# Last mixer's output projection: three of its four units with each 128-row product as two 64-row products in separate banks

## Chip, cores and metric

The kernel runs on one core of one Trainium2 chip. What counts is the time of one execution in microseconds (us), as the median of several. In the profile PE is TensorE's matmul stream and PEld its weight loads, DVE is VectorE, ACT ScalarE, POOL GpSimd, and SP the engine that issues the weight DMAs.

## What is computed

Three blocks run one after another on 512 tokens of width 1024, in f32: two of a first model (`even` mixer, FFN, `mla` mixer, FFN) and one of a second. The change is in the last mixer, of the second model:

```python
mix = jnp.concatenate([y_rwkv, o.reshape(B, S, DIFF_DIM)], axis=-1).astype(h.dtype)
h = h + rms_norm(mix @ w_out[l], ln_attn_post[l])
hn = rms_norm(h, ln_ffn_pre[l])
u = causal_dwconv(hn @ w_up[l], conv_w[l], conv_b[l])
gate, val = jnp.split(u, 2, axis=-1)
f = (jax.nn.gelu(gate, approximate=True) * val) @ w_down[l]
h = h + rms_norm(f, ln_ffn_post[l])
```

`mix @ w_out` is the output projection, 512 x 1024 by 1024 x 1024. The norm behind it needs the sum of squares over all 1024 features of a token, so nothing of the FFN can begin before the last column of the projection is there.

## The kernel before

Everything is held with features on the partitions: `XH` and `XL` are [128, 8 slices, 512 tokens]. A matrix product in f32 is made of three products in fp32r: weights and activations are each split into a high part and the rest, and `w_hi*XH + w_hi*XL + w_lo*XH` is summed in one PSUM bank. Weights come in units of 1 MB (`w_raw`, two slots): for the projection a unit is 1024 rows by 256 columns, so there are four units of two tiles (t = 0, 1) of 128 output features, and tiles n = 0 to 7 in all. One tile is 8 slices k times 3 factors = 24 products of 128 rows by 128 columns with 512 streamed tokens.

The order of the work is written out by hand, one program for each engine, with semaphores between them:

- SP loads unit u as soon as the low part of unit u - 2 is split off.
- ACT makes `w_hi` (L1036, 128x2048) of unit u + 1, once the unit's slot has been read (`read_of`), then takes the squares of the two tiles of unit u (`mean_square`, L1043), which wait for `lin_free`. In the last unit it makes one more high part between the two squares: the own weights of the FFN's second unit (`own_split`, L1080).
- DVE makes `w_lo` of unit u + 1 (L1582) from `w_hi`, then copies the two tiles of unit u from their banks to `Y2` (L2253) and raises `lin_free`. In the last unit its part of `own_split` (L2260) stands between the two copies.
- PE computes tiles 0 and 1 inside `group_norm` (L3298), then tiles 2 to 7 in `linear` (L2475), each through `feature_tile` (L2425), in banks L % 4, that is 0 to 3 by turns. `unit(u)` waits for `w_lo`, and `free(L)` for the bank.
- POOL adds the squares up (L886, L889), all but the last tile's.

Behind the last tile PE sums the squares over the partitions with a matrix of ones: L3093 for POOL's sum, L3095 for the last tile's squares. ACT turns this into `rstd` (L1084, L1085). DVE scales and adds the residual (L1970, L1973), ACT and DVE split the normed value (L1055, L1589), and PE begins the FFN (L2872). Eight records of L2861 ahead of it are four products that are never read.

Each engine takes its instructions in order, and ACT and DVE wait where they stand. The two lines around which the change is made:

```python
dve.wait_ge(lin_ready, L + 1)
dve.tensor_copy(Y2[:, n, :], bank[L % 4][:, :]).then_inc(lin_free, 1)
```

`side(h)` is a slice of 64 partitions: `side(0)` is 0 to 63, `side(1)` 64 to 127. Elsewhere the kernel has products on such halves in plain f32, among them L3113 in `lora_up`: 64 rows by 128 columns, 512 streamed, rows 0-63 and 64-127 by turns, each into another bank than the one before.

Of the kernel before, what the change touches and what calls it, by code (L numbers as in the profile page):

```python
# [13 lines left out]
ALU = mybir.AluOpType  # L14
AX = mybir.AxisListType

P = 128
SEQ = 512
D = 1024
KT = D // P  # L20
# [147 lines left out]
def build(nc, d, out, scratch, stages):  # L168
    units, first = units_of(stages, d)
# [17 lines left out]
    with ExitStack() as ctx:  # L187
        def sb(name, shape, dt=F32):
            return ctx.enter_context(nc.sbuf_tensor(name, shape, dt))

        def sem(name):
            return ctx.enter_context(nc.semaphore(name))

        bank = [ctx.enter_context(nc.psum_tensor(f"bank{i}", [P, 512], F32)) for i in range(8)]
# [6 lines left out]
        XH = sb("XH", [P, KT, SEQ], F32R)  # L201
        XL = sb("XL", [P, KT, SEQ], F32R)
# [82 lines left out]
        lin_ready = sem("lin_ready")  # L285
        lin_act = sem("lin_act")
        lin_free = sem("lin_free")
# [151 lines left out]
        Y2 = region(KT * SEQ, KT, SEQ)  # L439
# [170 lines left out]
        def wv(u, n, kt):  # L610

            return [w[:, u % 2, 0:kt * n].rearrange("p (t n) -> p t n", n=n) for w in (w_hi, w_lo)]
# [78 lines left out]
        def tok_units(stage):  # L691
            return [u for u in range(NU) if units[u][0] == stage]
# [32 lines left out]
        def side(h):  # L725
            return slice(CH * h, CH * (h + 1))
# [19 lines left out]
        inv = nc.dram_tensor("inverse_blocks", (3, P, BL * BL), F32, kind="Internal").ap()  # L746

        VAR, GATE = (4, 5), (6, 7)
        CENTRE = (4, 5, 7, 4)
        ABANK = (7, 5, 7, 6)  # L750
        PRE = (4, 5, 7, 4, 5, 7, 4, 5)
# [816 lines left out]
        def _(dve):  # L1568
# [7 lines left out]
            def split(u):  # L1576

                if u >= NU:
                    return
                dve.wait_ge(w_hi_ready, units_split(u + 1))  # L1580
                for (to, frm), (hi, _) in zip(split_pieces(u, w_raw, w_lo), split_pieces(u, w_raw, w_hi)):
                    last = dve.tensor_tensor(to, frm, hi.bitcast(F32), ALU.subtract)  # L1582
                last.then_inc(w_lo_ready, 1)
# [571 lines left out]
            def mix2():  # L2155
                L = lin_base["mix2"]
# [3 lines left out]
                for u in tok_units("rwkv_in"):  # L2160
# [15 lines left out]
                    for t in range(2):  # L2176
                        j = 2 * i + t
# [54 lines left out]
                for j in range(4):  # L2232
                    value(j)
                    dve.wait_ge(rw_vm, j + 1)
                    dve.scalar_tensor_tensor(vv[:, j, :], bank[CENTRE[j]][:, :], -1.0 / 64, vv[:, j, :],
                                             ALU.mult, ALU.add).then_inc(rw_vc, 1)
# [11 lines left out]
                for u in tok_units("mix_out"):  # L2248
                    split(u + 1)
                    for t in range(2):  # L2250
                        n = 2 * (u - first["mix_out"]) + t
                        dve.wait_ge(lin_ready, L + 1)
                        dve.tensor_copy(Y2[:, n, :], bank[L % 4][:, :]).then_inc(lin_free, 1)  # L2253
                        L += 1
                        if t == 0 and u == tok_units("mix_out")[-1]:
                            own_split(u + 2)
# [147 lines left out]
        def _(pe):  # L2404
# [60 lines left out]
            def free(L):  # L2465
                if L >= 4:
                    pe.wait_ge(lin_free, L - 3)

            def unit(u):
                pe.wait_ge(w_lo_ready, u + 1)  # L2470
# [4 lines left out]
            def linear(stage, L, release=False, late=None, skip=0):  # L2475

                for u in tok_units(stage)[skip:]:
                    unit(u)
                    for t in range(2):
                        free(L)  # L2480
                        if late and u == first[stage] and t == 0:
                            hi, lo = wv(u, 256, KT)
                            rows, name = late[1], late[0]
                            pe.wait_ge(ot_lo, ot_base[name] + min(rows.values()) - 1)
                            for p, k in enumerate([k for k in range(KT) if k not in rows] + list(rows)):
                                if k in rows:
                                    pe.wait_ge(ot_lo, ot_base[name] + rows[k])
                                for j, (w, x) in enumerate(((hi, XH), (hi, XL), (lo, XH))):
                                    m = pe.matmul(bank[L % 4][:, :], w[:, k, 0:P], x[:, k, :],
                                                  start=(p == 0 and j == 0), stop=(p == KT - 1 and j == 2))  # L2490
                            m.then_inc(lin_ready, 1)
                            L += 1
                            continue
                        m = feature_tile(u, KT, 256, whole(P * t), P, 0, L,
                                         release=release and t == 1 and u == tok_units(stage)[-1])
                        m.then_inc(lin_ready, 1)
                        L += 1
                return L
# [540 lines left out]
            def mix2():  # L3039
                L = lin_base["mix2"]  # L3040
                pe.wait_ge(down_added, down_base["ffn1"] + 4)
                for u in tok_units("rwkv_in"):
                    j = u - first["rwkv_in"]
                    unit(u)
                    if j == 0:
                        feature_pair(u, 256, (whole(0), whole(P)), L, "pre")
                        L += 2
                    else:
                        for t in range(2):
                            free(L)  # L3050
                            feature_tile(u, KT, 256, whole(P * t), P, 0, L).then_inc(lin_ready, 1)
                            L += 1
                            if j == 1 and t == 0:
                                pe.wait_ge(down_added, down_base["ffn1"] + KT)
                                pe.wait_ge(rstd_ready, norm_use["pre"])
                                pe.wait_ge(sq_mixed, 1)
                                pe.matmul(bank[5][:, :], C("ones"), sq_acc, start=True, stop=True).then_inc(ss_first, 1)
                                pe.matmul(bank[7][:, :], C("ones"), sq_acc2, start=True, stop=True).then_inc(ss_ready, 1)
                    if j == 2:
                        pe.wait_ge(first_rstd, 1)  # L3060
                        columns("pre")
                for u in tok_units("diff_in"):
                    j = u - first["diff_in"]
                    unit(u)
                    for t in range((2, 2, 2, 2, 4, 4)[j]):
                        free(L)
                        if j < 4:
                            feature_tile(u, KT, 256, whole(P * t), P, 0, L).then_inc(lin_ready, 1)
                            if t == 0 and j == 0:
                                lora_up()  # L3070
                            if t == 1:
                                key_sums(j)
                        else:
                            token_tile(u, KT, 256, lambda w, k: w[:, k, :], 256, 0, t, L).then_inc(lin_ready, 1)
                            if j == 4:
                                value_mean(t)
                            if j == 5 and t == 0:
                                pe.wait_ge(rw_vc, 4)
                            if j == 5 and t < 2:
                                inner(2 * t)  # L3080
                                inner(2 * t + 1)
                        L += 1
                    if j == 5:
                        pe.wait_ge(rw_ak, 4)
                pe.wait_ge(lin_free, L)
                pe.wait_ge(alibi_loaded, 16 * 16)
                attention("diff")
                rwkv_chunks()
                group_norm(L)
                linear("mix_out", L + 2, skip=1)  # L3090
                pe.wait_ge(rstd_ready, norm_use["post"])
                pe.wait_ge(sq_used, all_summed("post"))
                pe.matmul(bank[7][:, :], C("ones"), sq_acc, start=True, stop=False)  # L3093
                pe.wait_ge(sq_ready, LAST_POST + 1)
                pe.matmul(bank[7][:, :], C("ones"), squares[:, LAST_POST % 3, :], start=False, stop=True)\  # L3095
                    .then_inc(ss_ready, 1)

            def value_mean(t):
                if t == 2:
                    pe.wait_ge(rw_max, 4)  # L3100
                if t == 3:
                    pe.wait_ge(rw_vc, 1)
                pe.matmul(bank[CENTRE[t]][:, :], C("half_ones"), vv[:, t, :], start=True, stop=True).then_inc(rw_vm, 1)

# [220 lines left out]
            for j in range(3):  # L3325
                m = pe.transpose(bank[0][:, P * j:P * (j + 1)], vrow[:, j, :], ident)
# [34 lines left out]
```

## Time and profile before

| | us |
|---|---|
| median of 3 runs | 1925.27 |
| lowest, highest | 1925.08, 1927.24 |
| span of the profiled execution | 1924.0 |
| PE under way | 1890.1 (98%) |
| DVE busy | 999.1 (52%) |
| ACT busy | 740.1 (38%) |

For the profiled execution the span is given alone, from its first to its last instruction; what lies around it is not. The median of the runs is 1.3 us above it. The projection's tiles 2 to 7 run from 1511.40 to 1544.20 us of the span, and the FFN's first product starts at 1551.94. PE's busy time is that in which a product is under way: products overlap, so that the time shown for one is longer than the distance from one start to the next. Plain f32 products appear as two records each (two passes), fp32r ones as one.

### The profile page before, as it was taken

The numbers are of one execution on the slowest core, as the hardware profiler recorded it, in microseconds if no ns is written. First come the engines' busy times: TensorE is split into PE (matmuls) and PEld (weight loads), VectorE is DVE, ScalarE is ACT, GpSimd is POOL, SyncE is SP. The second block draws the span as 40 slices with busy tenths as digits, with TensorE's granted clock in tenths as the row PEclk, the third lists the DMA queues.
The fourth block names the chain that finished last, engine by engine and source line by source line (L and its number), as shares of the span: only waits on it lengthen the run. The fifth ranks groups of instructions, "written<-read, shape, count | busy, mean of one in ns | idle before, by whom it ended". The sixth has DMA issues, their size and how long they took to land.

```text
span 1924.0 us, 26779 instructions
## 1 busy us (share of the span) xinstructions
PE 1890.1 (98%) x10729; PEld 1527.6 (79%) x10729; DVE 999.1 (52%) x1418; ACT 740.1 (38%) x1111; POOL 179.1 (9%) x215
## 2 busy tenths in 40 slices
PE   9999999999999999999999999999999999999998
PEld 7875788888888777788888888777878778888887
DVE  5456453434325686553343434749563566656523
ACT  4247432222224575542222323554342454333322
POOL 1001210000001100010000000303551100000001
PEclk9999999999999999999999999999999999999999
DMA  6310133232322202123223232321120223232321
GB/s 201 105 44 1 50 99 98 87 109 87 105 92 80 72 23 66 45 91 105 91 87 109 88 109 87 100 88 44 24 67 25 88 77 109 87 108 89 107 90 66
DMA packets 137795, 158.74 MB, mean 83 GB/s; under 512 B 15976, under 2 KB 125552, under 8 KB 137712
## 3 DMA queue, kind: packets, MB, share of 16 engines
q1 hardware_dynamic: 136272, 155.01, 25.2%
q0 software_dynamic: 1440, 2.58, 0.5%
q8 instruction: 58, 0.95, 0.2%
q14 instruction: 25, 0.20, 0.0%
HBM read 153.89 MB, written 3.68 MB: 82 GB/s over the span
## 4 chain that ended last, share of the span: by engine, by line
PE 90%; DVE 6%; ACT 2%; issue 1%; DMA 0%; SPq 0%; POOL 0%; ACTq 0%; DVEq 0%
PE bank L2893 35%; PE bank L2926 16%; PE bank L2425 13%; PE bank L2450 3%; PE bank L2980 2%; PE bank L2569 2%; PE bank L2944 2%; PE bank L2839 1%; PE bank L2872 1%; PE bank L2597 1%; PE bank L2688 1%; PE bank L2584 1%; PE bank L2511 1%; PE bank L2541 1%; DVE XL L1589 1%
## 5 line engine op out<-in xcount | busy, mean ns | idle before, releaser
L2893 PE MATMUL bank<-XH,w_hi 128*128 128x512 f32 x992 | 386.8, 390 | 0.7 <-DVE arena L1889 0.7
L2893 PE MATMUL bank<-XL,w_hi 128*128 128x512 f32 x992 | 386.0, 389 | 0.0
L2893 PE MATMUL bank<-XH,w_lo 128*128 128x512 f32 x992 | 385.9, 389 | 0.0
L2893 PEld LDWEIGHTS bank<-XH,w_hi 128*128 128x128 f32 x992 | 186.2, 188 | 39.9 <-DVE arena L1889 0.9
L2893 PEld LDWEIGHTS bank<-XL,w_hi 128*128 128x128 f32 x992 | 186.2, 188 | 39.1 <-issue 0.5
L2893 PEld LDWEIGHTS bank<-XH,w_lo 128*128 128x128 f32 x992 | 186.2, 188 | 38.8
L2425 PE MATMUL bank<-XH,w_hi 128*128 128x512 f32 x448 | 178.7, 399 | 2.5 <-DVE w_lo L1582 2.4
L2425 PE MATMUL bank<-XH,w_lo 128*128 128x512 f32 x448 | 175.3, 391 | 0.0
L2425 PE MATMUL bank<-XL,w_hi 128*128 128x512 f32 x448 | 175.1, 391 | 0.0
L1582 DVE TENSOR_TENSOR w_lo<-w_raw,w_hi 128x2048 fp32r<-128x2048 f32 (+5 forms) x67 | 116.4, 1757 | 93.9 <-ACT w_hi L1036 93.5
L1936 DVE TENSOR_TENSOR w_lo<-w_raw,w_hi 128x2048 fp32r<-128x2048 f32 x24 | 55.0, 2292 | 174.2 <-ACT w_hi L1347 174.2
L1036 ACT ACTIVATE w_hi<-w_raw 128x2048 fp32r<-128x2048 f32 (+5 forms) x67 | 96.6, 1464 | 106.8 <-PE bank L2425 44.7
L2926 PE MATMUL bank<-XH,w_hi 128*128 128x512 f32 x320 | 124.5, 389 | 0.0
L2926 PE MATMUL bank<-XH,w_lo 128*128 128x512 f32 x320 | 124.5, 389 | 0.0
L2926 PE MATMUL bank<-XL,w_hi 128*128 128x512 f32 x320 | 124.5, 389 | 0.0
L1900 DVE TENSOR_TENSOR arena<-bank,arena 128x512 f32<-128x512 f32 x66 | 45.5, 690 | 141.0 <-PE bank L2893 141.0
L1291 ACT ACTIVATE w_hi<-w_raw 128x2048 fp32r<-128x2048 f32 x32 | 61.3, 1917 | 147.5 <-PE bank L2893 147.5
L1347 ACT ACTIVATE w_hi<-w_raw 128x2048 fp32r<-128x2048 f32 x24 | 46.0, 1917 | 187.1 <-PE bank L2926 166.5
L1876 DVE TENSOR_TENSOR w_lo<-w_raw,w_hi 128x2048 fp32r<-128x2048 f32 x33 | 75.6, 2290 | 62.9 <-ACT w_hi L1311 56.0
L2425 PEld LDWEIGHTS bank<-XH,w_hi 128*128 128x128 f32 x448 | 84.5, 189 | 25.1 <-DVE w_lo L1582 4.9
L2425 PEld LDWEIGHTS bank<-XL,w_hi 128*128 128x128 f32 x448 | 84.5, 189 | 18.9 <-issue 1.7
L2425 PEld LDWEIGHTS bank<-XH,w_lo 128*128 128x128 f32 x448 | 84.5, 189 | 17.8
(459 smaller groups left out, 3336.1 us busy)
## 6 DMA issues: line engine op xcount, KB each, us to landing
w_raw<-in_ffn_w_gate SPq DMA_DIRECT2D x22, 1024.0 KB, 5.3
w_raw<-in_ffn_w_up SPq DMA_DIRECT2D x22, 1024.0 KB, 5.3
w_raw<-in_ffn_w_down SPq DMA_DIRECT2D x22, 1024.0 KB, 4.9
w_raw<-in_w_up SPq DMA_DIRECT2D x22, 1024.0 KB, 5.1
w_raw<-in_w_in SPq DMA_DIRECT2D x13, 1024.0 KB, 5.3
w_raw<-in_w_down SPq DMA_DIRECT2D x11, 1024.0 KB, 5.0
w_raw<-in_even_w_in SPq DMA_DIRECT2D x8, 1024.0 KB, 5.3
w_raw<-in_even_w_out SPq DMA_DIRECT2D x4, 1024.0 KB, 5.3
```

The lines of the kernel that those rows point to most:

```text
L1036: last = act.activation(to, frm, ACT.Copy)
L1291: act.activation(w_hi[:, (u0 + 1) % 2, :], w_raw[:, (u0 + 1) % 2, :], ACT.Copy).then_inc(w_hi_ready, 1)
L1347: act.activation(w_hi[:, slot, :], w_raw[:, slot, :], ACT.Copy).then_inc(w_hi_ready, 1)
L1582: last = dve.tensor_tensor(to, frm, hi.bitcast(F32), ALU.subtract)
L1876: dve.tensor_tensor(w_lo[:, a, :], w_raw[:, a, :], w_hi[:, a, :].bitcast(F32), ALU.subtract).then_inc(w_lo_ready, 1)
L1900: dve.tensor_tensor(to[:, c, :], bank[2 + c][:, :], rstd, ALU.mult).then_inc(u_out, 1)
L1936: dve.tensor_tensor(w_lo[:, slot, :], w_raw[:, slot, :], w_hi[:, slot, :].bitcast(F32), ALU.subtract).then_inc(w_lo_ready, 1)
L2425: m = pe.matmul(bank[to][0:M, :], cols(w, k), x[:, x0 + k, :], start=(first_k and k == 0 and j == 0), stop=(last_k and k == kt - 1 and j = ...
L2450: m = pe.matmul(bank[to][:, 0:N], x[:, x0 + k, s * P:(s + 1) * P], cols(w, k), start=(k == 0 and j == 0), stop=(k == kt - 1 and j == 2))
L2569: pe.matmul(bank[SCORE[g % 4]][:, c:c + P * nk], qc[:, h, P * i:P * (i + 1)], kc[:, h, P * k0:P * (k0 + nk)], start=True, stop=True)
L2893: m = pe.matmul(bank[b][:, :], w[:, k, P * c:P * (c + 1)], x[:, k, :], start=(k == 0 and j == 0), stop=(k == KT - 1 and j == 2))
L2926: m = pe.matmul(bank[p][:, :], left, right, start=False, stop=(stop and c == 1 and j == 2))
```

## The change

For tiles 2 to 7 (the three units behind the first), `linear` gives way to `mix_out_halves`. Each product of 128 rows becomes two of 64: one on rows 0 to 63, into bank L % 4 as before, and one on rows 64 to 127, into a second bank (`LOWER`, 4, 5 or 6 by turns). The two orders of k and of the three factors are kept, and the two halves follow one another. DVE copies the upper half's bank to `Y2` and then adds the lower half's bank to it; between the two stands `link`, a wait of DVE for its own copy. `lin_free` is raised by the addition. From n = 5 on PE also waits until tile n - 3 has left its lower bank. Tiles 0 and 1 are as before.

```diff
+        LOWER = (4, 5, 6)
...
                         dve.wait_ge(lin_ready, L + 1)
-                        dve.tensor_copy(Y2[:, n, :], bank[L % 4][:, :]).then_inc(lin_free, 1)
+                        if n < 2:
+                            dve.tensor_copy(Y2[:, n, :], bank[L % 4][:, :]).then_inc(lin_free, 1)
+                        else:
+                            link(dve.tensor_copy(Y2[:, n, :], bank[L % 4][:, :]))
+                            dve.tensor_tensor(Y2[:, n, :], Y2[:, n, :], bank[LOWER[n % 3]][:, :], ALU.add)\
+                               .then_inc(lin_free, 1)
...
-                linear("mix_out", L + 2, skip=1)
+                mix_out_halves(L + 2)
...
+            def mix_out_halves(L):
+
+                for u in tok_units("mix_out")[1:]:
+                    unit(u)
+                    hi, lo = wv(u, 256, KT)
+                    for t in range(2):
+                        n = 2 * (u - first["mix_out"]) + t
+                        free(L)
+                        if n >= 5:
+                            pe.wait_ge(lin_free, L - 2)
+                        for k in range(KT):
+                            for j, (w, x) in enumerate(((hi, XH), (hi, XL), (lo, XH))):
+                                for r, to in ((side(0), L % 4), (side(1), LOWER[n % 3])):
+                                    m = pe.matmul(bank[to][:, :], w[r, k, P * t:P * (t + 1)], x[r, k, :],
+                                                  start=(k == 0 and j == 0), stop=(k == KT - 1 and j == 2))
+                        m.then_inc(lin_ready, 1)
+                        L += 1
```

On DVE, the program of before from tile 4's copy to the norm (the buffer `arena` holds `Y2`; L1582 is `w_lo` of the FFN's first unit, L2260 the own weights):

```order
L2253 COPY arena<-bank 128x512 x2
L1582 TENSOR_TENSOR w_lo<-w_raw,w_hi 128x2048
L2253 COPY arena<-bank 128x512
L2260 TENSOR_TENSOR under_arena<-w_raw,under_arena 128x2048
L2253 COPY arena<-bank 128x512
L1970 SCALAR_TENSOR_TENSOR arena<-arena,vec 128x512
```

and the changed program at the same place (its lines are 1 to 6 further down):

```order
L2257 COPY arena<-bank 128x512
L2258 TENSOR_TENSOR arena<-arena,bank 128x512
L2257 COPY arena<-bank 128x512
L2258 TENSOR_TENSOR arena<-arena,bank 128x512
L1583 TENSOR_TENSOR w_lo<-w_raw,w_hi 128x2048
L2257 COPY arena<-bank 128x512
L2258 TENSOR_TENSOR arena<-arena,bank 128x512
L2266 TENSOR_TENSOR under_arena<-w_raw,under_arena 128x2048
L2257 COPY arena<-bank 128x512
L2258 TENSOR_TENSOR arena<-arena,bank 128x512
L1971 SCALAR_TENSOR_TENSOR arena<-arena,vec 128x512
```

An addition stands behind each copy; nothing else has changed its place. On PE, the program of before where tile 1 ends and tile 2 begins:

```order
L3298 MATMUL bank<-XH,w_hi 128x512
L3298 MATMUL bank<-XL,w_hi 128x512
L3298 MATMUL bank<-XH,w_lo 128x512
L2425 MATMUL bank<-XH,w_hi 128x512
L2425 MATMUL bank<-XL,w_hi 128x512
L2425 MATMUL bank<-XH,w_lo 128x512
```

and the changed one (the shape is that of the output, 128 features by 512 tokens):

```order
L3322 MATMUL bank<-XH,w_hi 128x512
L3322 MATMUL bank<-XL,w_hi 128x512
L3322 MATMUL bank<-XH,w_lo 128x512
L3117 MATMUL bank<-XH,w_hi 128x512 x2
L3117 MATMUL bank<-XL,w_hi 128x512 x2
L3117 MATMUL bank<-XH,w_lo 128x512 x2
```

Each of the 144 rows of tiles 2 to 7 has become a pair at the same place.

## Rows read from the trace of the kernel before

**Rows 1.** The page, part 4: shares by engine of the chain that ended last

```profile
PE 90%; DVE 6%; ACT 2%; issue 1%; DMA 0%; SPq 0%; POOL 0%; ACTq 0%; DVEq 0%
```

**Rows 2.** That chain from 1505 to 1552: start us, us, what

```profile
1511.40 22.09 PE bank L2425 x96
...
1533.52 0.70 DVE arena L2253
...
1534.78 1.91 ACT w_hi L1036
...
1536.71 2.29 DVE w_lo L1582
...
1542.16 2.29 DVE under_arena L2260
...
1545.13 0.64 ACT arena L1043
...
1545.81 1.14 PE bank L3095 x2
```

**Rows 3.** Timeline of PE: start, us, line, operation, tiles, shapes, count [idle before <-releaser]

```profile
1543.74 0.39 PE L2425 MATMUL bank<-XL,w_hi 128*128 128x512 f32 x1
1543.97 0.40 PE L2425 MATMUL bank<-XH,w_lo 128*128 128x512 f32 x1
1544.20 1.02 PE L3093 MATMUL bank<-arena,con 128*128 128x512 f32 x2
1545.81 1.13 PE L3095 MATMUL bank<-arena,con 128*128 128x512 f32 x2 [0.59 <-ACT arena L1043]
1546.77 3.60 PE L2861 MATMUL bank<-con 128*128 128x512 f32 x8
1551.94 0.50 PE L2872 MATMUL bank<-XH,w_hi 128*128 128x512 f32 x1 [1.57 <-DVE XL L1589]
```

**Rows 4.** Timelines of PE and of PEld, the 64-row products of L3113

```profile
1287.32 1.98 PE L3113 MATMUL bank<-arena 64*128 64x512 f32 x6
...
1287.32 0.30 PEld L3113 LDWEIGHTS bank<-arena 64*128 64x128 f32 x4 [0.40 <-ACT arena L1444]
...
1289.69 0.29 PEld L3113 LDWEIGHTS bank<-arena 64*128 64x128 f32 x2 [1.22 <-ACT arena L1448]
```

**Rows 5.** Timeline of PE, and a window's row with PEclk, the granted clock

```profile
1212.47 0.50 PE L2425 MATMUL bank<-XH,w_hi 128*128 128x512 f32 x1 [1.79 <-DVE w_lo L1582]
...
1213.19 0.63 PE L2425 MATMUL bank<-XH,w_lo 128*128 128x512 f32 x1
...
1215.75 0.63 PE L2425 MATMUL bank<-XH,w_lo 128*128 128x512 f32 x1
...
1212.90:1216.20 3.30, 3.30 (x10) 2.52 (x9) 2.89 (x5) 3.01 (x5) 3.30 (x8) 0.50 0.81 236
```

**Rows 6.** DVE: a group, one line's min/median/max ns, and two timeline rows

```profile
L2253 DVE COPY arena<-bank 128x512 f32<-128x512 f32 x8 | 5.4, 689 | 9.4 <-PE bank L2425 9.4
...
L1900 DVE TENSOR_TENSOR arena<-bank,arena x66: 680/692/693, 278.1 to 1797.4; 128x512 f32<-128x512 f32 x66
...
1548.36 0.75 DVE L1970 SCALAR_TENSOR_TENSOR arena<-arena,vec 128x512 f32<-128x512 f32 x1 [3.26 <-ACT arena L1085]
1549.14 0.69 DVE L1973 TENSOR_TENSOR X<-X,arena 128x512 f32<-128x512 f32 x1
```

**Rows 7.** Timeline of PE at two other idle times

```profile
182.55 0.69 PE L2632 MATMUL bank<-con,arena 128*128 128x128 f32 x2 [2.70 <-POOL arena L910]
183.03 1.91 PE L2620 MATMUL bank<-arena 128*128 128x512 f32 x2
...
1337.24 1.13 PE L3121 MATMUL bank<-arena,con 128*128 128x512 f32 x2 [1.67 <-ACT arena L1457]
```

**Rows 8.** Timeline of PE and PEld within tile 6: a product and the next one's load

```profile
1534.90 0.39 PE L2425 MATMUL bank<-XL,w_hi 128*128 128x512 f32 x1
1534.90 0.19 PEld L2425 LDWEIGHTS bank<-XH,w_lo 128*128 128x128 f32 x1
```

## The prediction, made before the changed kernel ran

> **What bounds the kernel now.** I read the page first. TensorE (PE) holds 90% of the chain of work that ended last [rows 1], so PE's time in a stage is normally the stage's time, and the first question is what two half-height products cost in place of a full one. The second is which engine releases PE behind this stage, and there the page's average misleads. The chain in order of time [rows 2] shows that the projection is PE-bound only to tile 5: from 1511.40 the 96 products of tiles 2 to 5 take 22.09 us, 0.230 each. At 1533.52 the chain leaves PE. It then runs ACT and DVE by turns: DVE's copy of tile 5, ACT's square of it and its w_hi split, DVE's w_lo split, copy and square of tile 6, the two splits of the own weights (the second at 1542.16), copy and square of tile 7, and only then PE's L3095 at 1545.81. PE is busy all that time with tiles 6 and 7, but it ends them at the same moment as DVE ends L2260 (L3093, behind the last product, starts at 1544.20, and the split begun at 1542.16 ends 2.29 later, at 1544.45). So **two paths end level**: PE's last 48 products, and a serial walk over ACT and DVE. Behind L3095 comes the norm's chain (ACT, then DVE L1970, L1973, L1589), and PE's next real product starts at 1551.94 [rows 3].
>
> One product now starts every 0.227 us (1543.74, 1543.97, 1544.20 [rows 3]), though each is shown as 0.39 long, since records overlap.
>
> **Part 1, the products.** 144 products of 128 rows (3 units, 2 tiles, 8 slices, 3 factors) become 144 pairs with 64 rows each; the streamed columns, 512, stay. A 64-row product is no shorter than a 128-row one, so the pair costs what one did if both halves run at once, and twice that if they take turns. The trace has one place with this shape: L3113, 64 rows by 128 columns, 512 streamed, rows 0-63 and 64-127 by turns, in separate banks; it is in plain f32, so each product is two passes. Serial passes of this size: two take 1.02 us (L3093) and eight 3.60 (L2861), so one follows another after 0.43 and the last lasts 0.59 [rows 3]. The first three products of L3113, six passes, take 1.98 us [rows 4]. In series they would need 5 x 0.43 + 0.59 = 2.7 us before the first load; with the first two products at once they need 0.10 (load) + 3 x 0.43 + 0.59 = 1.98. The loads say the same: four of them cover 0.30 us, no more than the 0.29 of two loads for a lone product; one load is 0.19 [rows 8], so a second follows after 0.10. So the halves do run at once, loads too. What this place does not show is fp32r: there a column is streamed at twice the pace of a pass in f32 (0.227 against 0.43 for 512), and two banks would be written at that pace.
>
> I take a pair at 0.227, the value nearest to L3113. The low bound is 0.214 (half of the 0.427 between starts at half clock, six steps from 1213.19 to 1215.75 [rows 5]), the high bound for halves that do run together 0.24 (0.227 plus a second start some 0.01 behind). Only 96 pairs, those of tiles 2 to 5, lie on the path, as long as the walk over ACT and DVE is the longer one behind them: -1.3 to +1.3 us, taken as 0. Entering and leaving the half-array form may cost up to 0.18 (0.39 - 0.21, the tail of one product) once on the path; taken as 0.
>
> The Trainium skill (TensorE: Matmul & The Clock Gate, Part 3) puts it as a span of one matmul plus about 4 ns for each further tile, and says that a small-K matmul takes as long as a full one, the gain being concurrency alone. By that figure, an estimate, 96 pairs would add 0.4 us. No row here shows it for fp32r.
>
> **Part 2, the second bank's drain.** Tiles 2 to 7 now get a copy of one bank and then an addition of the other. The copy is 0.69 us and the addition too (L1900, same shape and sources, 692 ns); between an instruction and one that waits for its result lie 0.03 us (L1970 ends 1549.11, L1973 starts 1549.14) [rows 6]. So 0.72 us for each tile on DVE, 4.3 us in all. For tiles 2, 3 and 4 it is hidden: DVE idles 9.4 us in all ahead of two copies (those of tiles 3 and 5) [rows 6], and a w_lo split ends 5.5 us after its tile (1533.52 to 1536.71 + 2.29 [rows 2]), where PE's next unit wants it only after 48 x 0.227 = 10.9. For **tiles 5, 6 and 7 it is not hidden**, because ACT takes its work in order. ACT's square of tile 5 waits for the addition, the w_hi split stands behind the square, DVE's w_lo split waits for w_hi, tile 6's copy stands behind w_lo, and so on to L3095 [rows 2]. Each addition is one more link in that walk: 3 x 0.72 = **+2.2 us** at L3095. PE's level path gives it no cover; those 2.2 us are new idle time of PE. Counting only the last tile's addition would give +0.7, and would be wrong if the walk is as serial as the rows show.
>
> POOL's sum up to tile 6 is later by the same 1.5 us and still ends before PE comes to L3093. SP's load behind own_lo is later too, but PE has the first four FFN tiles ahead before it wants it. Both at nothing.
>
> **Part 3, the added wait.** From n = 5 on PE waits until tile n - 3 has left its lower bank. A tile lasts 5.4 us and DVE is behind by at most 2.2 us: the wait never holds. 0.
>
> **Part 4, PE's clock.** PE now idles 0.59 us ahead of L3095 [rows 3]; with part 2 it is 2.8 us. In this trace idle times of 1.79 us (before 1212.47) and 2.70 (before 182.55) went with a fall of the granted clock to 0.50, that is 1.2 GHz: the window behind the one shows it, and behind the other two f32 passes take 1.91 us. One of 1.67 us (before 1337.24) did not: two passes there take 1.13, a first load included [rows 5, 7]. So a fall here is more likely than not. What it costs: L3095 alone is on the path (the fill products L2861 end 1.57 us before L2872 needs PE), and its two f32 passes take 1.91 us at half clock (183.03) against 1.02: +0.9 if the fall covers them, 0 if it comes too late. I take half, +0.45.
>
> **The sum.** 0 + 2.2 + 0 + 0.45 = +2.6 us on the profiled span of 1924.0, or 1926.7. The median of the three runs is 1.3 above that span, which I carry over: **1927.9 us**. With the bounds (-1.3 to +1.3, 0 to 0.2, clock 0 to 0.9) this case spans 1926.2 to 1929.9. A measurement of this kernel can tell about 0.2% (3.9 us) from no change, so +2.6 us counts as "same".
>
> **Rivals.**
> *Halves in turn.* The fp32r halves do not overlap, for instance because the output path takes one full-speed stream only. Then a pair is 0.454 and the 144 pairs add 32.7 us; PE's path becomes the longer one, and only the last addition stands behind it (+0.7): 1925.3 + 33.4 = **1958.7, slower**. For it: L3113 streams at half this pace, so the trace has no pair at full pace. Against it: six passes in 1.98 us. It decides from 0.04 us more for each pair (96 x 0.04 = 3.8). This is also the case in which the change does not do what it says. 0.13.
> *Loads in turn.* Only the weight loads of the halves fall behind each other in full, 2 x 0.188 = 0.376 for a pair [rows 8]: 144 x 0.149 = 21.5, and +0.7: 1947.5. Against it: four loads in 0.30 us [rows 4]. Partial forms lie between 0.24 and 0.376; at 0.26 the sum is 1931. 0.07.
> *The pause between products goes.* If the 0.013 us between 0.227 and 0.214 are an unhidden bit of the weight swap, which two independent halves cover for one another, tile 5 is ready 96 x 0.013 = 1.3 us sooner: 1926.6. For it: twice 0.227 would be 0.454, and at half clock the step is 0.427 [rows 5], so the pause is no array time. Against it: each half swaps just as often. It lies inside the main case's bounds and is counted there.
> The Trainium skill (same page, Part 3) says that a weight load overlaps matmuls in flight only where the row groups differ, which would make the halves a gain. Here a full-height load starts together with a full-height product (both at 1534.90 [rows 8]), so the trace contradicts that as written.
> *Slack in the walk.* The additions at tiles 5 and 6 are absorbed, and only the last is paid: 1925.3 + 0.7 = 1926.0. Nothing in the rows offers that slack. 0.05.
> *A real gain* needs pairs under 0.164 us (96 x 0.063 = 6.0, less 2.2), below what 512 columns take at full clock. 0.02.
>
> **How the numbers follow.** Main case 0.73 (of it 0.06 above 1929.1, where bounds add up). Faster 0.02; slower 0.13 + 0.07 + 0.06 = 0.26; same 0.72. The range runs from 1925.8, under the slack case, to 1932, over the main case's top and the mild partial forms; it leaves out the serial cases.
>
> **What would show it.** Pairs: starts of the two halves within 0.01 us, pairs 0.227 apart, tile 5's copy still near 1533.5; 0.45 apart means the serial rival. Drain: six DVE additions of 0.69 us, ACT's w_hi at 1535.5, own_lo at 1543.6, the second ones product at 1548.0 instead of 1545.8, the first FFN product at about 1554.1 to 1555. Clock: a dip to 0.5 near 1547 to 1552. I am wrong if the fp32r halves are not concurrent, or if ACT's square does not stand between DVE's addition and the next split.

## The result and the profile after

| | before | changed |
|---|---|---|
| median of 20 runs, us | 1925.11 | 1927.57 |
| lowest, highest | 1922.21, 1927.24 | 1925.7, 1929.92 |
| span of the profiled execution | 1924.0 | 1926.0 |

The ratio is 1.0014, 95% interval 1.0009 to 1.002: the changed kernel is slower by 1.7 to 3.9 us, clearly there and under the 0.2% that count as a difference here. The forecast was 1927.9.

Spans differ by things that have nothing to do with the change, so the stage is read by itself. **S** is the time from the first product of tile 2 to the FFN's first product: 1511.40 to 1551.94 before, 40.54 us [rows 2, 3], and 1510.40 to 1554.00 in the changed kernel, 43.60. The stage is longer by 3.06 us. Behind S the spans have 372.1 and 372.0 us; ahead of it the changed kernel's execution is 1.0 us quicker, which is why its span is 2.0 and not 3.06 longer.

The chain that ended last in the changed kernel (start us, us, what; `...` stands for short pieces left out):

```profile
1510.40 22.12 PE bank L3117 x192
...
1532.54 0.70 DVE arena L2257
...
1533.26 0.70 DVE arena L2258
...
1534.52 1.91 ACT w_hi L1037
...
1536.46 2.29 DVE w_lo L1583
1538.75 0.61 DVE arena L2257
...
1539.39 0.70 DVE arena L2258
...
1540.65 1.92 ACT under_arena L1081
...
1542.58 2.29 DVE under_arena L2266
1544.88 0.61 DVE arena L2257
...
1545.51 0.70 DVE arena L2258
1546.21 0.02 issue
1546.23 0.64 ACT arena L1044
...
1546.92 2.09 PE bank L3101 x2
```

The first line answers the first of [rows 2]: 192 half products (96 pairs) in 22.12 us, where 96 whole ones took 22.09. From there the walk over DVE and ACT is that of before with three new pieces of 0.70 us (L2258). From tile 2's first product to the last ones product it was 34.41 us (1545.81 - 1511.40), and is 36.52.

PE's timeline at the same place, to be read against [rows 3], and a window's row (PEclk is the third last number):

```profile
1542.99 0.39 PE L3117 MATMUL bank<-XH,w_lo 64*128 64x512 f32 x2
1543.31 1.13 PE L3099 MATMUL bank<-arena,con 128*128 128x512 f32 x2
1546.92 2.08 PE L3101 MATMUL bank<-arena,con 128*128 128x512 f32 x2 [2.48 <-ACT arena L1044]
1548.78 4.12 PE L2867 MATMUL bank<-con 128*128 128x512 f32 x8
1554.00 0.50 PE L2878 MATMUL bank<-XH,w_hi 128*128 128x512 f32 x1 [1.09 <-DVE XL L1590]
...
1546.50:1549.80 3.30, 2.88 (x4) 1.34 (x5) 0.00 (x0) 1.10 (x3) 0.00 (x0) 0.50 0.90 306
```

PE comes to the first ones product 32.91 us after the stage's start (1543.31), before 32.80. Of the 0.11 us, 0.02 belong to the pairs (the last one starts after 32.59 us, the last whole product of before after 32.57) and 0.09 to the change back from halves: L3099 starts 0.32 behind the last pair, where 0.23 lay between the two before. PE then idles 2.48 us ahead of L3101 where it idled 0.59; the granted clock is 0.50 there, which is 1.2 GHz, and the two passes of L3101 take 2.08 us instead of 1.13. So the 3.06 us are 2.11 of walk (36.52 - 34.41) and 0.95 of clock.

The halves themselves, in the middle of a tile:

```profile
1512.14 0.40 PE L3117 MATMUL bank<-XL,w_hi 64*128 64x512 f32 x2
1512.38 0.39 PE L3117 MATMUL bank<-XH,w_lo 64*128 64x512 f32 x2
1512.60 0.40 PE L3117 MATMUL bank<-XH,w_hi 64*128 64x512 f32 x2
```

Each row holds two products, and the two together last 0.39 to 0.40, as one does. Pairs follow one another after 0.22 to 0.24.

### The profile page after: what moved, and what is told of

Its sections match the earlier page's. It is cut to its first block, busy times and chain, and to the rows that moved or that the text cites. A ratio compares the mean times of both kernels' runs of the same rounds, so it can differ in the third digit from the quotient of the medians.

```text
span 1926.0 us, 27075 instructions
## 1 busy us (share of the span) xinstructions
PE 1889.0 (98%) x10873; PEld 1525.7 (79%) x10873; DVE 1002.4 (52%) x1424; ACT 739.8 (38%) x1111; POOL 178.9 (9%) x215
## 4 chain that ended last, share of the span: by engine, by line
PE 90%; DVE 6%; ACT 2%; issue 1%; SPq 0%; DMA 0%; POOL 0%; DVEq 0%; ACTq 0%
PE bank L2899 35%; PE bank L2932 16%; PE bank L2431 12%; PE bank L2456 3%; PE bank L2986 2%; PE bank L2575 2%; PE bank L2950 2%; PE bank L3117 1%; PE bank L2845 1%; PE bank L2878 1%; PE bank L2603 1%; PE bank L2694 1%; PE bank L2590 1%; PE bank L2517 1%; PE bank L2547 1%
## 5 line engine op out<-in xcount | busy, mean ns | idle before, releaser
L2899 PE MATMUL bank<-XH,w_hi 128*128 128x512 f32 x992 | 386.8, 390 | 0.7 <-DVE arena L1890 0.7
L2899 PE MATMUL bank<-XH,w_lo 128*128 128x512 f32 x992 | 385.9, 389 | 0.0
L2899 PE MATMUL bank<-XL,w_hi 128*128 128x512 f32 x992 | 385.9, 389 | 0.0
L2899 PEld LDWEIGHTS bank<-XH,w_hi 128*128 128x128 f32 x992 | 186.2, 188 | 39.8 <-DVE arena L1890 0.9
L2899 PEld LDWEIGHTS bank<-XL,w_hi 128*128 128x128 f32 x992 | 186.2, 188 | 39.2 <-issue 0.5
L2899 PEld LDWEIGHTS bank<-XH,w_lo 128*128 128x128 f32 x992 | 186.2, 188 | 38.7
L2431 PE MATMUL bank<-XH,w_hi 128*128 128x512 f32 x400 | 159.4, 398 | 2.5 <-DVE w_lo L1583 2.4
L2431 PE MATMUL bank<-XH,w_lo 128*128 128x512 f32 x400 | 155.8, 390 | 0.0
L2431 PE MATMUL bank<-XL,w_hi 128*128 128x512 f32 x400 | 155.8, 390 | 0.0
L2932 PE MATMUL bank<-XH,w_hi 128*128 128x512 f32 x320 | 124.5, 389 | 0.0
L2932 PE MATMUL bank<-XH,w_lo 128*128 128x512 f32 x320 | 124.5, 389 | 0.0
L2932 PE MATMUL bank<-XL,w_hi 128*128 128x512 f32 x320 | 124.5, 389 | 0.0
L1901 DVE TENSOR_TENSOR arena<-bank,arena 128x512 f32<-128x512 f32 x66 | 45.5, 690 | 141.0 <-PE bank L2899 141.0
L1301 ACT ACTIVATE arena<-arena 128x512 f32<-128x512 f32 x44 | 27.6, 631 | 180.9 <-DVE arena L1886 180.9
L1886 DVE TENSOR_TENSOR arena<-bank,arena 128x512 f32<-128x512 f32 x44 | 30.2, 691 | 127.6 <-PE bank L2899 116.4
L2431 PEld LDWEIGHTS bank<-XH,w_hi 128*128 128x128 f32 x400 | 75.1, 188 | 22.6 <-DVE w_lo L1583 4.4
```

The costliest lines, as they stand in the source:

```text
L1901: dve.tensor_tensor(to[:, c, :], bank[2 + c][:, :], rstd, ALU.mult).then_inc(u_out, 1)
L2431: m = pe.matmul(bank[to][0:M, :], cols(w, k), x[:, x0 + k, :], start=(first_k and k == 0 and j == 0), stop=(last_k and k == kt - 1 and j = ...
L2899: m = pe.matmul(bank[b][:, :], w[:, k, P * c:P * (c + 1)], x[:, k, :], start=(k == 0 and j == 0), stop=(k == KT - 1 and j == 2))
L2932: m = pe.matmul(bank[p][:, :], left, right, start=False, stop=(stop and c == 1 and j == 2))
```

## The experiments

All are changes of one of the two kernels. S and the length of the idle time ahead of the last ones product are read from each one's profiled execution, before rounding, so that two of the rounded times here can give 0.01 us more or less; times are medians, the ratio is to the kernel before on the same chip. In the table "walk" is the time from tile 2's first product to the last ones product, and "clock" whether it fell to 0.50 there.

| run | S, us | walk, us | PE idle, us | clock | ratio, 95% interval |
|---|---|---|---|---|---|
| before | 40.54 | 34.41 | 0.59 | | |
| changed | 43.60 | 36.52 | 2.48 | fell | 1.0014, 1.0009 to 1.002 |
| e1_halves_no_add | 40.55 | 34.43 | 0.39 | | 1.0000, 0.9991 to 1.001 |
| e2_add_only | 43.53 | 36.46 | 2.66 | fell | 1.0014, 1.0004 to 1.0023 |
| e3_add_early | 40.51 | 34.39 | 0.59 | | 1.0004, 0.9995 to 1.0014 |
| e5_add_last | 41.24 | 35.12 | 1.31 | | one run, 1924.54 |
| e6_act_order | 41.27 | 35.14 | 1.11 | | 1.0002, 0.9992 to 1.0011 |
| e7_fill | 42.61 | 36.48 | 0.77 | | 1.0009, 0.9999 to 1.0018 |
| e8_square_from_bank | 39.75 | 33.64 | none | | 0.9991, 0.9981 to 1.0001 |
| e4_grouped | 65.66 | 59.53 | 1.11 | | one run, 1950.38 |
| e9_blocks_3 | 42.62 | 36.49 | 2.49 | | one run, 1927.13 |
| e10_blocks_6 | 43.33 | 37.20 | 2.47 | | one run, 1928.84 |

**The two parts apart.** Theory: the pairs are free and the additions are the whole cost. Rival: the pairs cost. First the pairs alone, the changed kernel with

```diff
-                        if n < 2:
-                            dve.tensor_copy(Y2[:, n, :], bank[L % 4][:, :]).then_inc(lin_free, 1)
-                        else:
-                            link(dve.tensor_copy(Y2[:, n, :], bank[L % 4][:, :]))
-                            dve.tensor_tensor(Y2[:, n, :], Y2[:, n, :], bank[LOWER[n % 3]][:, :], ALU.add)\
-                               .then_inc(lin_free, 1)
+                        dve.tensor_copy(Y2[:, n, :], bank[L % 4][:, :]).then_inc(lin_free, 1)
```

> The changed kernel without the six additions: DVE copies the upper half's bank alone, so the output lacks the lower 64 rows of every product of tiles 2 to 7. PE's work is that of the changed kernel. Stretch S = from the first product of tile 2 to the first FFN product (L2872 or its like): 40.54 us before, 43.60 changed. Theory (the pairs are free, the additions on the walk over ACT and DVE cost all): S = 40.5 to 40.7, no clock fall at the norm, time within 0.1% of before. Rival (the pairs themselves cost, through loads or ports): S stays above 42.5.

S is 40.55 us, before's within 0.01, and the time ratio 1.0000. Then the second DVE instruction alone, the kernel before with

```diff
-                        dve.tensor_copy(Y2[:, n, :], bank[L % 4][:, :]).then_inc(lin_free, 1)
+                        if n >= 2:
+                            link(dve.tensor_copy(Y2[:, n, :], bank[L % 4][:, :]))
+                            dve.tensor_tensor(Y2[:, n, :], Y2[:, n, :], bank[L % 4][:, :], ALU.max)\
+                               .then_inc(lin_free, 1)
+                        else:
+                            dve.tensor_copy(Y2[:, n, :], bank[L % 4][:, :]).then_inc(lin_free, 1)
```

> The kernel before with 128-row products, and behind the copies of tiles 2 to 7 the same link and a second DVE instruction of the addition's form (max of Y2 and the same bank, which leaves Y2 as it is). Theory: S = 40.54 + 3 x 0.72 = 42.7 us, or up to 43.6 where the granted clock falls ahead of the ones product; time 2.2 to 3.1 us over before. Rival (the pairs cost): S = 40.6, no difference in time.

S is 43.53 us with PE's products untouched: the whole difference, and the same ratio as the changed kernel, 1.0014. PE shows the same picture, idle time and slow passes included:

```profile
1543.18 1.02 PE L3098 MATMUL bank<-arena,con 128*128 128x512 f32 x2
1546.86 2.08 PE L3100 MATMUL bank<-arena,con 128*128 128x512 f32 x2 [2.66 <-ACT arena L1043]
```

What e2 lacks of the halves' picture is the change back from them. In the changed kernel the first ones product starts 0.09 us later behind the last tile's products, and shows 1.13 us for its two passes where L3098 shows 1.02. The 0.20 us come off the idle time that follows (2.48 against 2.66, and 0.39 in e1 against 0.59 before), so nobody waits for them.

**Where an added instruction costs.** Theory: it is a link of the walk from tile 5 on, and hidden before. Rival: it costs wherever it stands. As e2, with `if 2 <= n < 5:`, then with `if n == 7:`.

> As e2_add_only, but the second DVE instruction behind the copies of tiles 2, 3 and 4 alone. Theory (these are hidden in DVE's idle time, since tile 5's copy waits for PE): S = 40.5, time as before. Rival (each DVE instruction in the stage costs wherever it stands): S = 40.54 + 2.2 = 42.7.

> The kernel before with the second DVE instruction (the max that leaves Y2 as it is) behind tile 7's copy alone. Theory (each one from tile 5 on is one link of the walk): stretch S from the first product of tile 2 to the first FFN product = 40.54 + 0.72 = 41.26 us; the first product with ones of the last tile's squares 1.31 us behind PE's last work instead of 0.59. Rival (what costs is the PE clock, or any added instruction costs the same 2.2 to 3): S = 42.5 or more.

Behind tiles 2 to 4 three such instructions cost nothing: S 40.51, against 42.7 by the rival. DVE's timeline shows how they vanish:

```profile
1522.47 0.69 DVE L2254 COPY arena<-bank 128x512 f32<-128x512 f32 x1 [3.95 <-PE bank L2430]
1523.20 0.69 DVE L2255 TENSOR_TENSOR arena<-arena,bank 128x512 f32<-128x512 f32 x1
1526.39 2.29 DVE L1582 TENSOR_TENSOR w_lo<-w_raw,w_hi 128x2048 fp32r<-128x2048 f32 x1 [2.51 <-ACT w_hi L1036]
1528.60 0.68 DVE L2254 COPY arena<-bank 128x512 f32<-128x512 f32 x1
1529.32 0.69 DVE L2255 TENSOR_TENSOR arena<-arena,bank 128x512 f32<-128x512 f32 x1
1533.35 0.69 DVE L2258 COPY arena<-bank 128x512 f32<-128x512 f32 x1 [3.35 <-PE bank L2430]
```

The w_lo split behind tile 3 is late by what was added (it begins 3.92 us after tile 3's copy, before 3.20), but tile 5's copy still waits 3.35 us for PE, and there the delay ends. Behind tile 7 one instruction costs 0.70 us (S 41.24, expected 41.26). Both as the theory has it. The time of e3 cannot tell 0 from 2 us: its interval reaches to 1.0014.

**ACT's place in the walk.** The changed kernel, with ACT's order in the stage turned so that no split stands behind a square that waits for an addition:

```diff
                 for u in tok_units("mix_out"):
                     split(u + 1)
-                    for t in range(2):
-                        mean_square("post", 2 * (u - first["mix_out"]) + t)
-                        if t == 0 and u == tok_units("mix_out")[-1]:
-                            own_split(u + 2)
+                    if u > first["mix_out"]:
+                        mean_square("post", 2 * (u - first["mix_out"]) - 1)
+                    if u == tok_units("mix_out")[-1]:
+                        own_split(u + 2)
+                    mean_square("post", 2 * (u - first["mix_out"]))
+                mean_square("post", KT - 1)
```

> The changed kernel with ACT's order turned: the w_hi split of the next unit and the own weights' high part come ahead of the square of the tile before, so that no split waits for an addition. The arithmetic is the same. Theory (the cost of tiles 5 and 6 comes from ACT's place in the walk): both splits leave the path, tile 7's copy starts at once when PE is done, only the last addition is left: S = 41.3 us, no clock fall or a rarer one, time 0.7 us over before. Rival (DVE's added work itself is what is late): S = 42.7 to 43.6 as in the changed kernel.

S falls from 43.60 to 41.27, the walk from 36.52 to 35.14. The chain now stays on PE to the stage's end:

```profile
1511.82 32.99 PE bank L3119 x288
...
1544.84 0.70 DVE arena L2259
...
1545.56 0.70 DVE arena L2260
1546.26 0.02 issue
1546.28 0.64 ACT arena L1044
...
1546.96 1.14 PE bank L3103 x2
```

DVE has all six additions still; two of the three that cost are hidden again by the order of ACT alone, and what is left, 41.27, is what one addition behind tile 7 costs by itself (e5, 41.24). This is the experiment that shows the mechanism: what made an addition dear was who stood behind it on another engine.

**The clock.** The changed kernel with two useless products (four passes) behind the first ones product:

```diff
                 pe.matmul(bank[7][:, :], C("ones"), sq_acc, start=True, stop=False)
+                pe.wait_ge(lin_free, L + 2 + KT - 4)
+                for _ in range(2):
+                    pe.matmul(bank[6][:, :], ident, con[:, 0:512], start=True, stop=True)
                 pe.wait_ge(sq_ready, LAST_POST + 1)
```

> The changed kernel with two products of no use (ident by constants, into bank 6, four passes, 1.7 us) behind the first ones product, in the idle time of 2.5 us. Theory (idle time there drops the clock, and that costs 0.95 of the 3.06 us): no fall to 0.50 ahead of the ones product, S = 43.60 - 0.95 = 42.65 us; time 0.5 to 1 us under the changed kernel. Rival (the fall comes from something else, such as the 64-row products): the fall is still there, S = 43.6.

```profile
1542.91 1.88 PE L3102 MATMUL bank<-con 128*128 128x512 f32 x4
1545.56 1.12 PE L3104 MATMUL bank<-arena,con 128*128 128x512 f32 x2 [0.77 <-ACT arena L1044]
...
1541.90:1551.60 9.70, 7.45 (x18) 2.88 (x16) 6.33 (x9) 3.78 (x6) 0.00 (x0) 1.00 0.33 110
```

The clock stays at 1.00, the two passes take 1.12 and S is 42.61, as expected. The walk is that of the changed kernel (36.48 against 36.52), so the 0.95 us are the clock's. The rival of the expectation, that the 64-row products bring the fall, is out by e2, which has the fall with whole products only. But one execution does not prove that the fill products prevented it: e9 and e10 below idle as long as the changed kernel (2.49 and 2.47 us) without a fall. Of four profiled executions with some 2.5 us of idle time there, two had it (changed, e2) and two not.

The clock averaged over the whole span is on record for every run and says more. A fall as long as the one at the norm lowers it by 0.001: e9's execution and the changed kernel's both have a fall near 185 us, e9's has no other and 0.998, the changed kernel's has the one at the norm besides and 0.997. Of the 20 runs of the changed kernel none has 0.998 or more, and of the 10 of e2 none. Of the kernel before, 13 of 25 have it on e2's chip and 12 of 25 on e7's, and of e7 5 of 10. Had only every second run of the changed kernel and of e2 a fall at the norm, half of a half, some 7 of the 30, should still be at 0.998 or more. So the fall is probably in most of their runs, and the fill probably keeps it away, since e7 has such runs as often as before. This is an estimate: the averages do not show where a run's falls lie. Why e9 and e10 escaped is open. The time of e7 (1.0009, 0.9999 to 1.0018) does not tell it from the changed kernel's either.

**Are the halves really side by side?** The other reading of pairs that take 0.227 us is that a half-height product takes half the time by itself. The changed kernel with the loops turned, so that all of a tile's products on one side come first:

```diff
-                        for k in range(KT):
-                            for j, (w, x) in enumerate(((hi, XH), (hi, XL), (lo, XH))):
-                                for r, to in ((side(0), L % 4), (side(1), LOWER[n % 3])):
+                        for r, to in ((side(0), L % 4), (side(1), LOWER[n % 3])):
+                            for k in range(KT):
+                                for j, (w, x) in enumerate(((hi, XH), (hi, XL), (lo, XH))):
```

> The changed kernel with the loops turned: all 24 products of a tile on rows 0 to 63 first, then all 24 on rows 64 to 127. The same 288 products and loads. Theory (a 64-row product lasts as long as a 128-row one, and halves gain only by lying side by side): a tile takes 48 x 0.227 = 10.9 us, S = 40.5 + 32.7 + 0.7 = 73.9, time 1958.7 us. Rival (a half-height product costs half by itself, order is nothing): S = 43.6, time as the changed kernel.

A lone 64-row product is as long as a whole one, 0.227 us from start to start, and the kernel takes 1950.38 us. The second reading is out. But the theory missed the size: S is 65.66 us, not 73.9, and a tile 9.38, not 10.9. The trace shows why, here where tile 2's lower half gives way to tile 3's upper one:

```profile
1518.87 0.39 PE L3117 MATMUL bank<-XL,w_hi 64*128 64x512 f32 x1
1519.10 0.39 PE L3117 MATMUL bank<-XH,w_lo 64*128 64x512 f32 x1
1519.10 0.60 PE L3117 MATMUL bank<-XH,w_hi 64*128 64x512 f32 x2
1519.44 0.50 PE L3117 MATMUL bank<-XL,w_hi 64*128 64x512 f32 x2
1519.67 0.49 PE L3117 MATMUL bank<-XH,w_lo 64*128 64x512 f32 x2
1519.90 0.39 PE L3117 MATMUL bank<-XH,w_hi 64*128 64x512 f32 x1
```

Around each change of side some products lie beside others: 57.29 us from the stage's first product to L3099, 252 steps of 0.227 for 288 products, so 36 saved at 11 changes of side, 3.3 at each. One product of the next group beside the last of this one would save one. So products of the other side must start before earlier ones of this side: in the second and third row one starts at 1519.10 together with the XH,w_lo that is fourth from its group's end, while the three behind that one still come. Two runs put that to the test, the changed kernel with blocks of 3 and of 6:

```diff
-                        for k in range(KT):
-                            for j, (w, x) in enumerate(((hi, XH), (hi, XL), (lo, XH))):
-                                for r, to in ((side(0), L % 4), (side(1), LOWER[n % 3])):
-                                    m = pe.matmul(bank[to][:, :], w[r, k, P * t:P * (t + 1)], x[r, k, :],
-                                                  start=(k == 0 and j == 0), stop=(k == KT - 1 and j == 2))
+                        sides = ((side(0), L % 4), (side(1), LOWER[n % 3]))
+                        for i, s in [(i, s) for b in range(0, 24, 3) for s in range(2) for i in range(b, b + 3)]:
+                            k, j = divmod(i, 3)
+                            (w, x), (r, to) = ((hi, XH), (hi, XL), (lo, XH))[j], sides[s]
+                            m = pe.matmul(bank[to][:, :], w[r, k, P * t:P * (t + 1)], x[r, k, :],
+                                          start=(i == 0), stop=(i == 23))
```

> The changed kernel with the halves in blocks of 3: three products on rows 0 to 63, then the same three on rows 64 to 127, and so on. In the grouped form (blocks of 24) the trace showed some 3.4 products lying beside others at each change of side, and a tile of 9.38 us. Theory (PE may start a product of the other half up to 3 or 4 places ahead of its turn): blocks of 3 are as good as pairs, tile 5.44 us, S = 43.6 us. Rival (products start strictly in the order of the program, and the overlap at a change of side is a thing of the change alone): only the last of a block lies beside the first of the next, a block pair takes 4 or 5 instead of 3 steps of 0.227, tile 7.3 to 9 us, S of 55 to 65.

> As e9_blocks_3 with blocks of 6. Theory (a reach of 3 to 4 places): each change of side saves about 3.4 steps, so two blocks of 6 take 12 - 6.8 = 5.2, which 6 bounds from below if the reach carries on, or about 8.6 if it saves once for each change of side at its own start: tile 5.44 to 7.8 us, S of 43.6 to 58. Rival (strict order): 11 steps for two blocks of 6, tile 10 us, S about 70.

Blocks of 3 are as good as pairs: 32.88 us to the first ones product, against 32.91 (S is 42.62 because the clock did not fall). Blocks of 6 take 33.60, three steps more in the whole stage (their S of 43.33 lies under the expected 43.6 because here too the clock did not fall). Their first products show the reach:

```profile
1511.59 0.50 PE L3118 MATMUL bank<-XH,w_hi 64*128 64x512 f32 x1
1511.93 0.40 PE L3118 MATMUL bank<-XL,w_hi 64*128 64x512 f32 x1
1512.17 0.39 PE L3118 MATMUL bank<-XH,w_lo 64*128 64x512 f32 x1
1512.18 0.62 PE L3118 MATMUL bank<-XH,w_hi 64*128 64x512 f32 x2
1512.52 0.52 PE L3118 MATMUL bank<-XL,w_hi 64*128 64x512 f32 x2
```

In the program the first six products are on the upper side: XH,w_hi; XL,w_hi; XH,w_lo; and the same three of the next slice. Yet right behind the third, 0.01 us later, one with XH,w_hi starts. It can't be the fourth, which would follow the third on the same rows after 0.23. It is the seventh, the first of the lower side. It stands **four places behind the third in the program and starts right after it, ahead of the fourth, fifth and sixth**. From there on the two sides run level, with the lower one behind by what it lost at the start. The rival (strict order) gave S of 55 to 70 for these two and is out. Strict order was what the Trainium skill says of matmuls (TensorE: Matmul & The Clock Gate, Part 3); these rows contradict it for products on different halves. The reach seen is four places, for fp32r with 512 columns. No run shows more: in e10 nothing of the lower side started beside the first or the second product, which stand six and five places ahead of the seventh, and blocks of 24 save no more than some 3.3 steps at a change of side. What sets the limit is not shown.

**A version against both.** The kernel before, with ACT taking the square of tile 7 straight from its bank and DVE's copy behind it:

```diff
-                        mean_square("post", 2 * (u - first["mix_out"]) + t)
+                        p = 2 * (u - first["mix_out"]) + t
+                        if p == KT - 1:
+                            last = lin_base["mix2"] + LIN_TILES["mix2"]
+                            act.wait_ge(lin_ready, last)
+                            square(LAST_POST, bank[(last - 1) % 4][:, :], 1.0 / 32)
+                        else:
+                            mean_square("post", p)
...
                         dve.wait_ge(lin_ready, L + 1)
+                        if n == KT - 1:
+                            dve.wait_ge(sq_ready, LAST_POST + 1)
                         dve.tensor_copy(Y2[:, n, :], bank[L % 4][:, :]).then_inc(lin_free, 1)
```

> A version meant to beat both: the kernel before, but ACT takes the square of tile 7 straight from its PSUM bank, and DVE's copy of it follows the square. It takes the copy (0.66 us) out of the path between PE's last product and the norm. Theory: the last ones product starts at about 1545.2 where it started at 1545.81 (0.66 earlier relative to tile 2's first product), S = 39.9 us, time 0.6 us under before, less than a measurement can tell. Rival (the walk of splits is still as long as PE, so nothing is won): S = 40.5.

```profile
1542.74 1.02 PE L3101 MATMUL bank<-arena,con 128*128 128x512 f32 x2
1543.60 1.12 PE L3103 MATMUL bank<-arena,con 128*128 128x512 f32 x2
1544.55 3.60 PE L2869 MATMUL bank<-con 128*128 128x512 f32 x8
```

The walk is 33.64 us and S 39.75, 0.79 less than before; the two ones products now follow one another without idle time (1542.74 + 2 x 0.43 = 1543.60). The time, 1923.75 us, is the lowest of all medians, and the ratio 0.9991 with an interval of 0.9981 to 1.0001: in the stage the gain is seen, in the whole it isn't proved.

## Why the prediction was right

*Two paths level, then a walk over ACT and DVE.* The frame of the whole forecast. Shown: e3 and e5 place the cost, e6 takes two thirds of it away by the order of ACT.

*Part 1, pairs at 0.227, 96 of them on the path, taken as 0.* Measured +0.03 us (22.12 against 22.09), and e1 gives S within 0.01. The bounds of 1.3 us either way were far too wide. The bridge from L3113's plain f32 to fp32r held, although L3113 streams at half the pace. The 4 ns for a further tile that the Trainium skill gives (TensorE: Matmul & The Clock Gate, Part 3), 0.4 us over 96 pairs, is not seen. That a small-K matmul takes as long as a full one stands on that page under "Why this matters for your kernels" and not in Part 3; e4's lone halves, 0.227 us from start to start, agree. The change of form was put at up to 0.18 and is 0.20 (0.09 until the first ones product starts, 0.11 in its length), on PE's side, where nobody waits for it. What entering it costs isn't seen, because PE waits for w_lo just there.

*Part 2, 3 x 0.72 = 2.2.* Measured 2.11 on the walk, 2.05 in e2. The three pieces are there in full; the copies of tiles 6 and 7 are shown 0.05 us shorter than before (0.61 against 0.66).

*Part 3, the added wait, 0.* The last pair starts 32.59 us after the first with the wait, and the last whole product of before after 32.57, so it never held.

*Part 4, the clock, +0.45 as half of 0.9.* The fall came in the profiled execution and cost 0.95, on an idle time of 2.48 us and not 2.8. Two falls in four profiled executions would bear out the half, but the averaged clocks of the runs make a fall in most of them likelier. The term was then too low by up to half a microsecond: walk and clock together are 3.06 us in the stage, where the sum has 2.6.

*The number.* That 1927.9 lies 0.3 us beside the median of 1927.57 is in part luck. The interval of the ratio, 1.7 to 3.9 us, would hold a sum with no clock term (2.2) as well as one with the whole of it (3.1), and the 1.3 us from span to median that were carried over came from three runs.

*Rivals.* Halves in turn (1958.7) and loads in turn (1947.5) fell with the first row of the trace. The pause between products did not go: pairs keep 0.227, in e4 lone halves too, so a product beside another one does not cover it. There was no slack in the walk: three additions cost 2.11 us, not one's 0.7.

*Not foreseen.* I had priced the serial rival, with no overlap at all, at 33.4 us; a kernel written to run its halves in turn (e4) loses only 25.1 in S, because PE reaches ahead. The forecast of e4 was wrong by 8 us for that reason.

## What to carry to other kernels

Splitting a product that already fills the array's height buys nothing: both halves run at once, each as long as the whole (0.227 us from start to start), and what is new is a second bank to drain. Ask of each instruction added to a drain not how long it is but what stands behind it: here three of six cost their full 0.72 us. Two did so because a square that waited for them stood in front of the next weights' split on ACT, and a change of ACT's order freed them; the third because the norm itself waits for it. Where two paths end level, lengthening one costs in full, and what is worth cutting is the piece behind both, as e8 did (0.79 us). That cutting one path alone would gain nothing follows from the picture, but no run here does it.

## What the runs showed of the hardware

- Products on different halves of the array's rows may start ahead of their turn: in e10 the seventh starts right behind the third, ahead of three that stand before it. So they needn't be interleaved one by one: blocks of 3 cost nothing, blocks of 6 cost 0.7 us in a stage of 33, blocks of 24 cost 24.4.
- fp32r halves into two banks run at the full pace of 0.227 us for 512 columns.
- After some 2.5 us of idle time PE's clock was at 1.2 GHz in two of four profiled executions, at 0.95 us for two plain f32 passes (2.08 for 1.13). The same idle time need not end the same way: 1.79 us before 1212.47 had a fall in the profile of before, 1.80 us before 1211.94 none in that of the changed kernel.
- Runs of one kernel scatter by 4 to 5 us. Falls of the clock elsewhere come and go between executions: the profile of before has them at 182, 206 and 1213 us of the span, the changed kernel's only the first of these, near 185; the granted clock is 1.00 there from 204 to 214 and from 1211 to 1217. That fits its being 1.0 us quicker ahead of the stage, and is why S was read instead of the span. On the chip of e7 the runs of before with an average clock of 0.995 took 1926.7 us in the mean, those with 0.998 1924.3.
